# Gate and up projections as one wide product with the high and low halves of x side by side; x loaded first, relative bias by a row-shifted copy in DRAM

## The chip, the cores and the metric

One core of one Trainium2 chip runs the whole program. The metric is the device time of one execution in microseconds, the median of several; lower is better. A difference of under about 0.2% is not one that these measurements tell.

## The reference

Two transformer stacks one after the other on x of 256 tokens by 1024: `first_block` with two layers, `second_block` with one. Six times in all a SwiGLU feed-forward layer runs, and it is most of the work:

```python
x = x + 0.5 * swiglu(rmsnorm(x, g), w_gate, w_up, w_down)   # 1024 -> 2816 -> 1024
```

Between them stand a short convolution with sliding-window attention, a block attention (MoBA) whose 256 keys here are one own block, two cross attentions on a memory of 256 rows that is normed once, a convolution module with gated linear attention, and a last gated projection. Two of the attentions add a relative bias, `table[bucket(query - key)]`, by head.

## The kernel before

**Weights.** All of them stream from DRAM once, in units of 1 MB (`units`, 256 columns or 256 rows of a matrix), into three raw slots. Every unit is two halves. ACT copies a half to `w_hi` (`split`, L480, type fp32r), and DVE subtracts that from the raw values to `w_lo` (`split`, L837); six halves fit in `w_hi` and `w_lo`. Activations are kept the same way, as `xT_hi`, `xT_lo`. A product is three matmuls, hi·hi, hi·lo and lo·hi (`products`, L1347), so that the lost part of each operand is made good. SP issues the load of a unit when `lo_ready` says that the unit three before has been split. ACT may write a half when the half six before it has been used (`half_done`).

**A feed-forward layer** (`ffn`, L1487; `ffn_step` on ACT and DVE) has 11 steps j of 256 hidden columns. For each, PE makes two halves of gate and two of up (`gate_up`, `transposed`): output is hidden by tokens, 128x256 for a half, 24 matmuls of 256 columns. Then it makes the down product of the step before (`down`, `row_half`, 24 matmuls of 512 columns). Both halves of gate share one PSUM bank, as do both of up, and the banks alternate with j, so a step never waits for the last one's results. Steps 2 to 9 are a loop of two steps. DVE multiplies the bank by the scale of the norm (L945 gate, L950 up), ACT applies silu (L537), DVE multiplies both (L954), ACT and DVE make `hid_hi` (L541) and `hid_lo` (L959). The first step of a layer is an `opening`: K tiles 0 to 3 of all four halves first, then 4 to 7, since the tail of x is still being made. After the last step `last_rows` ends the sums one by one; DVE adds each to x (L924), and PE transposes x (L1433) for the next norm. The fifth layer is `late`: x is normed twice first (`final_norm`, L905), and PE broadcasts the scale (`scale_broadcast`, L1482) after the first half of step 1.

**The start.** SP issues the first gate unit, then x, then up and gate; ACT issues gains, table, memory and a few small loads. ACT splits two halves, then makes `xT_hi` (L508), squares x (L492), and splits the next halves. The memory is normed after step 0. After step 1 PE transposes all gain vectors (`memory_and_vectors`, L1565 to L1567) and the memory (L1574), and ACT and DVE make `memT`. Then `relative_bias` reverses the rows of a bias read from DRAM by a matmul with a flipped identity (L1591); DVE copies that out (L981), and only then does the first down product start.

```python
for n, (l, r) in enumerate(((0, 0), (0, 1), (1, 0))):
    last = pe.matmul(dst, lhs[l], rhs[r], start=start and n == 0, stop=stop and n == 2,
```

## Time and profile before

| | |
|---|---|
| median of 3 runs | 1677.15 us (1676.81 to 1677.82) |
| profiled execution, its own time | 1675.95 us |
| its span | 1674.2 us |
| DVE, ACT, POOL busy | 62%, 45%, 4% |
| weight loads of PE (PEld) busy | 89% |
| granted clock of PE, mean | 0.989 |
| moved by DMA | 280.16 MB, 167 GB/s |

Busy PE is the time in which at least one matmul was in flight; matmuls overlap, so the pace of a stream is read from the starts of neighbours in the timeline and not from the duration of one. The chain of waits names the work that set the end. Lines are those of the kernel before.

### The profile page before, as it was taken

What the parts mean: (1) busy time and instruction counts of PE and PEld (TensorE: products, weight loads), DVE (VectorE), ACT (ScalarE), POOL (GpSimd) and SP (SyncE); (2) the same over time, 40 slices, a digit from 0 to 9 for tenths busy, and PEclk for the clock granted to TensorE, in tenths of its full rate; (3) what the DMA queues carried; (4) which work ended last, traced back from release to release, by engine and by line L of the source; (5) the groups of instructions that cost most, each with busy time, mean ns of one, the idle gap of its engine ahead of it and who ended that gap; (6) DMA issues with size and microseconds to landing.
All of it is one profiled execution on the core that took longest, in us unless ns stands there. A gap on an engine that the chain in (4) does not pass through costs nothing.

```text
span 1674.2 us, 27810 instructions
## 1 busy us (share of the span) xinstructions
PE 1612.6 (96%) x11185; PEld 1496.9 (89%) x11185; DVE 1031.4 (62%) x1472; ACT 757.0 (45%) x1009; POOL 70.9 (4%) x142
## 2 busy tenths in 40 slices
PE   6899999999999999999998999999999999999997
PEld 6799989799999899999977999998999898899995
DVE  5655557767555665656466755566555886755565
ACT  4444435445444444444454544444444641544444
POOL 3000001000000000000000800000000000000000
PEclk9999989999999999999999999999999999999999
DMA  7555543535556555555442456546565450456561
GB/s 266 175 179 186 178 138 127 175 126 162 191 178 198 176 183 179 188 181 175 151 159 93 151 176 200 175 159 213 175 200 163 151 176 26 140 194 200 175 206 45
DMA packets 207748, 280.16 MB, mean 167 GB/s; under 512 B 5135, under 2 KB 183721, under 8 KB 207417
## 3 DMA queue, kind: packets, MB, share of 16 engines
q1 hardware_dynamic: 205184, 273.17, 50.1%
q0 software_dynamic: 1040, 3.28, 0.6%
q10 hardware_dynamic: 1448, 2.65, 0.5%
q8 instruction: 54, 0.88, 0.2%
q14 instruction: 22, 0.17, 0.0%
HBM read 276.98 MB, written 2.11 MB: 167 GB/s over the span
## 4 chain that ended last, share of the span: by engine, by line
PE 86%; DVE 10%; ACT 3%; issue 1%; DMA 1%; DVEq 0%; ACTq 0%; SPq 0%
PE bank L1347 79%; DVE w_lo L837 4%; PE bank L1755 2%; PE bank L1433 1%; PE bank L1554 1%; ACT w_hi L480 1%; PE bank L1536 1%; ACT xT_hi L508 1%; DMA x<-in_x 1%; DVE x L924 0%; PE bank L1543 0%; DVE arena L1031 0%; DVE xT_lo L877 0%; PE bank L1591 0%; PE bank L1482 0%
## 5 line engine op out<-in xcount | busy, mean ns | idle before, releaser
L1347 PE MATMUL bank<-xT_hi,w_hi 128*128 128x256 f32 x2512 | 717.9, 286 | 6.1 <-DVE w_lo L837 4.6
L1347 PE MATMUL bank<-xT_lo,w_hi 128*128 128x256 f32 x2512 | 713.1, 284 | 0.0
L1347 PE MATMUL bank<-xT_hi,w_lo 128*128 128x256 f32 x2512 | 713.0, 284 | 0.0
L480 ACT ACTIVATE w_hi<-raw 128x1024 fp32r<-128x1024 f32 x518 | 531.7, 1052 | 289.6 <-PE bank L1347 249.1
L837 DVE TENSOR_TENSOR w_lo<-raw,w_hi 128x1024 fp32r<-128x1024 f32 x518 | 614.4, 1223 | 70.6 <-ACT w_hi L480 70.3
L1347 PEld LDWEIGHTS bank<-xT_hi,w_hi 128*128 128x128 f32 x2512 | 484.3, 193 | 13.9 <-issue 5.9
L1347 PEld LDWEIGHTS bank<-xT_lo,w_hi 128*128 128x128 f32 x2512 | 484.4, 193 | 2.5
L1347 PEld LDWEIGHTS bank<-xT_hi,w_lo 128*128 128x128 f32 x2512 | 484.2, 193 | 0.0
L1347 PE MATMUL bank<-w_hi,hid_hi 128*128 128x512 f32 x528 | 207.9, 394 | 0.8 <-DVE bias L981 0.8
L1347 PE MATMUL bank<-w_lo,hid_hi 128*128 128x512 f32 x528 | 206.2, 391 | 0.0
L1347 PE MATMUL bank<-w_hi,hid_lo 128*128 128x512 f32 x528 | 205.6, 389 | 0.0
L945 DVE TENSOR_TENSOR arena<-bank,scale_row 128x512 f32<-128x512 f32 x66 | 45.6, 691 | 245.8 <-PE bank L1347 245.6
L950 DVE TENSOR_TENSOR arena<-bank,scale_row 128x512 f32<-128x512 f32 x66 | 45.5, 690 | 159.7 <-PE bank L1347 159.7
L541 ACT ACTIVATE hid_hi<-arena 128x512 fp32r<-128x512 f32 x66 | 41.8, 633 | 193.5 <-DVE arena L954 193.5
L1347 PEld LDWEIGHTS bank<-w_hi,hid_lo 128*128 128x128 f32 x528 | 99.2, 188 | 21.1
L1347 PEld LDWEIGHTS bank<-w_hi,hid_hi 128*128 128x128 f32 x528 | 99.4, 188 | 19.9 <-DVE bias L981 1.6
L1347 PEld LDWEIGHTS bank<-w_lo,hid_hi 128*128 128x128 f32 x528 | 99.4, 188 | 17.8
L537 ACT ACTIVATE arena<-arena 128x512 f32<-128x512 f32 x66 | 41.8, 633 | 157.9 <-DVE arena L945 157.9
L1347 PE MATMUL bank<-w_hi,yT_hi 128*128 128x512 f32 x136 | 55.1, 405 | 6.7 <-DVE yT_lo L1045 6.7
L877 DVE SCALAR_TENSOR_TENSOR xT_lo<-bank,cols,xT_hi 128x256 fp32r<-128x256 f32 x88 | 36.4, 477 | 38.8 <-ACT xT_hi L508 38.8
L1347 PE MATMUL bank<-w_hi,yT_lo 128*128 128x512 f32 x136 | 53.1, 390 | 0.0
L1347 PE MATMUL bank<-w_lo,yT_hi 128*128 128x512 f32 x136 | 53.0, 390 | 0.0
(242 smaller groups left out, 1301.6 us busy)
## 6 DMA issues: line engine op xcount, KB each, us to landing
raw<-in_ffn_w_gate SPq DMA_DIRECT2D x44, 1024.0 KB, 5.4
raw<-in_ffn_w_up SPq DMA_DIRECT2D x44, 1024.0 KB, 5.6
raw<-in_ffn_w_down SPq DMA_DIRECT2D x44, 1024.0 KB, 5.0
raw<-in_ffn_w_in SPq DMA_DIRECT2D x44, 1024.0 KB, 5.2
raw<-in_ffn_w_out SPq DMA_DIRECT2D x22, 1024.0 KB, 5.0
raw<-in_w_in SPq DMA_DIRECT2D x10, 1024.0 KB, 5.3
raw<-in_xa_w_kv SPq DMA_DIRECT2D x8, 1024.0 KB, 5.2
raw<-in_od_w_in SPq DMA_DIRECT2D x8, 1024.0 KB, 5.5
```

Of the source, the lines that this page charges most:

```text
L480: act.activation(hi, src, ACT.Copy).then_inc(sem["hi_ready"], 1)
L508: last = act.activation(hi[:, k, :], src, ACT.Copy, scale=gain_of(gain, k))
L537: act.activation(act_gate[:, jb, :], act_gate[:, jb, :], ACT.Silu).then_inc(sem["act_gate_ready"], 1)
L541: act.activation(hid_hi[:, 2 * jb:2 * jb + 2, :], hidden[:, jb, :].rearrange("p (s t) -> p s t", s=2), ACT.Copy).then_inc(sem["hidden_hi_r ...
L837: dve.tensor_tensor(lo, src, hi.bitcast(F32), ALU.subtract).then_inc(sem["lo_ready"], 1)
L877: last = dve.scalar_tensor_tensor(lo[:, k, :], src, gain_of(gain, k), hi[:, k, :].bitcast(F32), ALU.mult, ALU.subtract)
L945: dve.tensor_tensor(halves(act_gate[:, jb, :]), halves(bank[:, 2 * jb, :]), both, ALU.mult)\
L950: dve.tensor_tensor(halves(hidden[:, jb, :]), halves(bank[:, 2 * jb + 1, :]), both, ALU.mult)\
L1347: last = pe.matmul(dst, lhs[l], rhs[r], start=start and n == 0, stop=stop and n == 2, skip_group_check=shared)
L1433: last = pe.transpose(bank[:, k, t * P:(t + 1) * P], x[:, t, k * P:(k + 1) * P], ident[:, :])
L1536: last = pe.matmul(bank[:, g, n * nk:(n + 1) * nk], q_of(h, t), k_of(h, nk), start=True, stop=True)
L1755: last = pe.matmul(bank[:, b, 0:T], tap_diag(tile, j), glu[:, tile, j:j + T], start=j == 0, stop=j == CONV_TAPS - 1)
```

## The change

- `xT_hi` and `xT_lo` become two parts of one buffer `xT` (K tile by part by token), so that both halves of a K tile are 512 adjacent columns. A half of gate or up gets a PSUM bank of its own (n = 0 to 3, no alternation with j). `wide` multiplies `w_hi` of all eight K tiles by the 512 columns, then `w_lo` of all eight by the 256 of `xT_hi`, into the right side of the bank. It waits for `hi_ready` first and for `lo_ready` only before the low part.
- ACT copies the right sides of two banks to `gate_part` and `up_part`, DVE adds the left sides (`gate_sum`, `up_sum`) and then scales. PE waits for `gate_summed` of the step before ahead of half 0, and for `up_summed` ahead of half 2. The splits stand at other places among these instructions.
- `opening` uses `wide_product` (512 and 256 columns by K tile). In the first layer `wide` is used instead, K tiles as x comes in.
- x is loaded first, in two parts, and the first gate unit in two; the memory is loaded on SP after the first up unit. One split instead of two comes before the first norm. The memory is squared and scaled before step 0, and transposed before step 1.
- The other gain vectors are transposed at the end of the first layer (`vectors`), and DVE takes them out after `hid_lo` of its last step (`vector_columns`).
- The bias: POOL copies the spread table in DRAM to 128 rows, each one element further (`shift_dram`), and reads it back strided, once for each attention. Flip, reversal and store are gone.

```diff
+        xT = sb("xT", [P, KD, 2, T], F32R)
+        xT_hi, xT_lo = xT[:, :, 0, :], xT[:, :, 1, :]
...
+            for t, name in enumerate(("x_loaded", "x1_loaded")):
+                sp.dma_start(x[:, t, :], a["x"][0].rearrange("(t p) d -> p t d", p=P)[:, t, :]).then_inc(sem[name], 16)
...
+            pool.dma_start(bass.AP(shift_dram.tensor, 0, [[8 * 512 + 1, P], [512, 8], [1, 384]]),
+                           bass.AP(spread_dram.tensor, 0, [[0, P], [384, 8], [1, 384]])).then_inc(sem["spread_shifted"], 16)
+            pool.wait_ge(sem["spread_shifted"], 16)
+            by_distance = shift_dram[:, :, P - 1:P - 1 + T]
+            pool.dma_start(bias[:, :, :], by_distance).then_inc(sem["bias_loaded"], 16)
...
+                def gate_low():
+                    act.wait_ge(sem["half_done"], plus(g_half + 2, LOOP_HALVES))
+                    act.activation(gate_part[:, :, :], bank[:, 0:2, T:2 * T], ACT.Copy).then_inc(sem["gate_part_ready"], 1)
...
+                gate_low()
+                if j == 0:
+                    up_low()
+                    silu()
+                else:
+                    split(i, base + 2)
+                    silu()
+                    split(i, base + 3)
+                    up_low()
...
                 if j == 0:
                     split(i, base)
+                    gate_sum()
+                    split(i, base + 1)
+                    up_sum()
                     scale_copy(4)
+                    gate_scale()
+                    up_scale()
...
-                ffn_step(f, NJ - 1)
+                ffn_step(f, NJ - 1, after_hidden=vector_columns if n_ffn[0] == 1 else None)
...
-            splits(2)
+            split()
             norm(COL_OF["ffn1"], loaded=True)
-            splits(LEAD - 2)
+            splits(LEAD - 1)
+            memory_scale()
...
+            def wide(v, b, i, first=False):
+
+                pe.wait_ge(sem["hi_ready"], v + 1 if i is None else v + 1 + LOOP_HALVES * i)
+                for k in range(KD):
+                    if first:
+                        c.next("xT_lo_ready")
+                    pe.matmul(bank[:, b, :], w_cols(v, k)[0], xT[:, k, :, :], start=k == 0, stop=False)
+                split_ready(v, i)
+                for k in range(KD):
+                    last = pe.matmul(bank[:, b, T:2 * T], w_cols(v, k)[1], xT_hi[:, k, :], start=False, stop=k == KD - 1)
                 last.then_inc(sem["half_done"], 1)
...
-                        transposed(v + n, gate_up_dst(j, n), X, i)
+                        if n in (0, 2):
+                            ready = j0 + j
+                            pe.wait_ge(sem["up_summed" if n else "gate_summed"], ready if i is None else ready + 2 * i)
+                        wide(v + n, n, i)
...
+                if n_ffn[0] == 1:
+                    memory()
                 gate_up(1)
                 if n_ffn[0] == 1:
-                    memory_and_vectors()
-                    relative_bias()
+                    c.next("xT_lo_ready", 4)
...
                 down(NJ - 2, v0 + 6 * (NJ - 1) + 2)
+                if n_ffn[0] == 1:
+                    vectors()
                 down(NJ - 1, v0 + FFN_HALVES - 2)
```

How PE's rows move in the loop body, first half of gate of a step. Before (six of its 24 rows; the pattern repeats by K tile):

```order
L1347 MATMUL bank<-xT_hi,w_hi 128x256 [waits lo_ready]
L1347 MATMUL bank<-xT_lo,w_hi 128x256
L1347 MATMUL bank<-xT_hi,w_lo 128x256
L1347 MATMUL bank<-xT_hi,w_hi 128x256
L1347 MATMUL bank<-xT_lo,w_hi 128x256
L1347 MATMUL bank<-xT_hi,w_lo 128x256
```

The three matmuls of a K tile stand together, and the half waits for `w_lo`. Now, the whole half:

```order
L1452 ISA [waits gate_summed]
L1456 MATMUL bank<-xT,w_hi 128x512 [waits hi_ready]
L1456 MATMUL bank<-xT,w_hi 128x512 x7
L1459 MATMUL bank<-xT,w_lo 128x256 [waits lo_ready]
L1459 MATMUL bank<-xT,w_lo 128x256 x7
```

Eight matmuls of 512 columns and eight of 256 take the place of 24 of 256; the half now waits for a sum of DVE.

DVE in the loop body of the change, one step from its first split (L971 and L975 are the sums, L979 and L983 the scalings, L1004 the product of gate and up, L1007 `hid_lo`):

```order
L863 TENSOR_TENSOR w_lo<-raw,w_hi 128x1024 [waits hi_ready]
L970 ISA
L971 TENSOR_TENSOR arena<-bank,arena 128x512 [waits gate_part_ready]
L861 REGISTER_ALU
L863 TENSOR_TENSOR w_lo<-raw,w_hi 128x1024 [waits hi_ready]
L979 TENSOR_TENSOR arena<-arena,scale_row 128x512 [waits gate_summed]
L861 REGISTER_ALU
L863 TENSOR_TENSOR w_lo<-raw,w_hi 128x1024 [waits hi_ready]
L975 TENSOR_TENSOR arena<-bank,arena 128x512 [waits up_part_ready]
L983 TENSOR_TENSOR arena<-arena,scale_row 128x512 [waits up_summed]
L1004 TENSOR_TENSOR arena<-arena 128x512 [waits act_gate_ready,up_scaled]
L1007 TENSOR_TENSOR hid_lo<-arena,hid_hi 128x512 [waits hidden_hi_ready]
```

Six instructions of 128x512 stand where there were four, and the third and fourth split now stand ahead of the sum of up, where they stood behind the product of gate and up.

PE in the first layer, between step 1 and the first down product. Before:

```order
L1565 MATMUL bank<-ident,gain_row 128x1 [waits gain_loaded,vectors_loaded]
L1565 MATMUL bank<-ident,gain_row 128x1 x7
L1566 MATMUL bank<-ident,arena 128x128
L1567 MATMUL bank<-ident,arena 128x126
L1574 MATMUL bank<-ident,arena 128x128 [waits scale_ready,cols_ready,mem_normed]
L1574 MATMUL bank<-ident,arena 128x128 x15
L1591 MATMUL bank<-arena 128x512 [waits bias_rev_loaded,xT_lo_ready]
L1591 MATMUL bank<-arena 128x512 x3
L1347 MATMUL bank<-w_hi,hid_hi 128x512 [waits lo_ready,hidden_lo_ready,bias_ready]
```

In the change the sixteen memory transposes stand ahead of step 1, and the last row is:

```order
L1394 MATMUL bank<-w_hi,hid_hi 128x512 [waits lo_ready,hidden_lo_ready,xT_lo_ready]
```

The rows of L1591 are gone, and those of the gain vectors have moved to the end of the layer, ahead of its last down product.

## Rows read from the trace of the kernel before

**Rows 1.** Page, part 1: busy time of PE, share of the span, instructions.

```profile
PE 1612.6 (96%) x11185; PEld 1496.9 (89%) x11185; DVE 1031.4 (62%) x1472; ACT 757.0 (45%) x1009; POOL 70.9 (4%) x142
```

**Rows 2.** Timeline, PE, a loop step: start, duration in us; 21 and 54 matmuls apart.

```profile
430.06 0.39 PE L1347 MATMUL bank<-w_hi,hid_lo 128*128 128x512 f32 x1
...
434.83 0.39 PE L1347 MATMUL bank<-w_hi,hid_lo 128*128 128x512 f32 x1
...
436.01 0.28 PE L1347 MATMUL bank<-xT_hi,w_lo 128*128 128x256 f32 x1
...
442.49 0.28 PE L1347 MATMUL bank<-xT_hi,w_lo 128*128 128x256 f32 x1
```

**Rows 3.** Timeline, PE, at the start, before the clock rose; six matmuls apart.

```profile
14.22 0.41 PE L1347 MATMUL bank<-xT_hi,w_lo 128*128 128x256 f32 x1
...
15.50 0.42 PE L1347 MATMUL bank<-xT_hi,w_lo 128*128 128x256 f32 x1
```

**Rows 4.** Timeline, DVE, a loop step of the third layer; in brackets what it waited for.

```profile
602.79 0.69 DVE L950 TENSOR_TENSOR arena<-bank,scale_row 128x512 f32<-128x512 f32 x1 [2.46 <-PE bank L1347]
...
614.62 2.35 DVE L837 TENSOR_TENSOR w_lo<-raw,w_hi 128x1024 fp32r<-128x1024 f32 x2
...
619.77 0.69 DVE L950 TENSOR_TENSOR arena<-bank,scale_row 128x512 f32<-128x512 f32 x1 [2.80 <-PE bank L1347]
```

**Rows 5.** Timeline, ACT, the same step.

```profile
616.89 1.06 ACT L480 ACTIVATE w_hi<-raw 128x1024 fp32r<-128x1024 f32 x1 [0.57 <-PE bank L1347]
...
621.23 0.63 ACT L541 ACTIVATE hid_hi<-arena 128x512 fp32r<-128x512 f32 x1 [3.27 <-DVE arena L954]
```

**Rows 6.** Timeline, DVE, then PE, end of the first layer.

```profile
209.72 0.69 DVE L950 TENSOR_TENSOR arena<-bank,scale_row 128x512 f32<-128x512 f32 x1 [2.80 <-PE bank L1347]
...
217.42 1.28 DVE L924 SCALAR_TENSOR_TENSOR x<-bank,x 128x512 f32<-128x512 f32 x2
...
218.16 0.66 PE L1433 MATMUL bank<-ident,x 128*128 128x128 f32 x4 [0.29 <-DVE x L924]
```

**Rows 7.** Chain of waits from 0 to 60 us: start, duration in us, what.

```profile
1.32 8.80 DMA x<-in_x
...
16.61 1.16 ACT arena L492 x2
...
21.64 8.93 PE bank L1347 x60
...
31.01 12.94 PE bank L1347 x108
...
43.95 0.59 PE bank L1565 x8
...
50.56 5.25 PE bank L1591 x8
...
56.59 3.47 PE bank L1347 x14
```

**Rows 8.** Busy time by engine from 15 to 20 us; the last two: DMA share, GB/s.

```profile
15.00:20.00 5.00, 2.85 (x20) 2.65 (x18) 3.07 (x16) 4.10 (x8) 5.00 (x11) 1.00 1.09 361
```

**Rows 9.** Timeline, PE, the memory's transposes.

```profile
45.67 1.94 PE L1574 MATMUL bank<-ident,arena 128*128 128x128 f32 x16 [0.76 <-issue]
```

**Rows 10.** Timeline, ACT and then DVE, in the first 45 us.

```profile
12.52 3.02 ACT L508 ACTIVATE xT_hi<-bank,cols 128x256 fp32r<-128x256 f32 x8 [4.02 <-PE bank L1433]
...
41.65 1.42 DVE L1051 TENSOR_SCALAR arena<-arena,small 128x1024 f32<-128x1024 f32 x2
```

**Rows 11.** Timeline, DVE, then PE, steps 0 and 1 of the fifth layer.

```profile
1132.20 1.22 DVE L837 TENSOR_TENSOR w_lo<-raw,w_hi 128x1024 fp32r<-128x1024 f32 x1
...
1132.34 0.70 PE L1482 MATMUL bank<-diag,unit_sq 128*128 128x256 f32 x2 [1.01 <-DVE diag L896]
...
1139.86 0.39 PE L1347 MATMUL bank<-xT_hi,w_hi 128*128 128x256 f32 x1 [0.37 <-DVE w_lo L837]
```

**Rows 12.** Page, part 6: issues of a weight unit, KB each, us to landing.

```profile
raw<-in_ffn_w_gate SPq DMA_DIRECT2D x44, 1024.0 KB, 5.4
```

More of the change, by code:

```diff
@@ L65 @@
 N_COLS = _at
+FIRST_COLS = 24
 def bucket_starts():
@@ L955, in ffn_step @@
                     .then_inc(sem["hidden_ready"], 1)
-                for n in range(2, 4 if j else 2):
-                    split(i, base + n)
                 dve.wait_ge(sem["hidden_hi_ready"], plus(f.j0 + j + 1, 2))
@@ L977, in ffn @@
                 if n_ffn[0] == 1:
-                    memory_norm()
-                    for n in range(4):
-                        c.next("bias_psum")
-                        dve.tensor_copy(bias[:, 2 * n:2 * n + 2, :], halves(bank[:, 4 + n, :]))\
-                            .then_inc(sem["bias_ready"], 1)
+                    xT_los(COL_OF["mem"], memT_hi, memT_lo, by_bank=True)
                 if n_ffn[0] == 6:
@@ L1357, in _, with opening @@
             X, Y, MEM, HID = (xT_hi, xT_lo), (yT_hi, yT_lo), (memT_hi, memT_lo), (hid_hi, hid_lo)
-            def opening(parts, before_last=None, loaded=False):
-                for n, (v, dst, start) in enumerate(parts):
+            def opening(vs, product, before_last=None):
+                for n, v in enumerate(vs):
                     split_ready(v, None)
-                    if n == 2 and not loaded:
+                    if n == 2:
                         rest_of_x()
@@ L1368, in opening @@
                             c.next("xT_lo_ready")
-                        products(dst, w_cols(v, k), xk(X, k), start and k == 0, False, shared=True)
-                for n, (v, dst, _) in enumerate(parts):
-                    if n == len(parts) - 1 and before_last is not None:
+                        product(n, k)
+                for n in range(len(vs)):
+                    if n == len(vs) - 1 and before_last is not None:
                         before_last()
```

191 lines of the change are left out of this document (108 added, 83 removed), and 2 rows, old and new, of the table AX.

## The prediction

> **What bounds the kernel now.** I read the page's busy times first: PE has a matmul in flight for 1612.6 of 1674.2 us [rows 1], so time can come from two places only, a faster stream of matmuls or the few stretches in which PE stands. The timeline of PE gives the stream's pace. Twenty-one matmuls of 512 columns take 434.83 - 430.06 = 4.77 us, 227.1 ns each; fifty-four of 256 columns take 442.49 - 436.01 = 6.48 us, 120.0 ns each [rows 2]. At 2.4 GHz the columns alone need 213.3 and 106.7 ns. So either length pays about 13.5 ns over its columns. At the start, with the granted clock at 1.2 GHz, six matmuls of 256 take 1.28 us, 213.3 ns each, which is the columns and nothing more [rows 3]. A step of a layer lasts 619.77 - 602.79 = 16.98 us [rows 4], and 96 x 0.1200 + 24 x 0.2271 = 16.97 us accounts for it: in the loop PE never waits, and DVE and ACT wait for it [rows 4, 5].
> The chain of the first 60 us shows the other place. x lands at 10.12; two squares on ACT end at 17.77; PE takes up its third half at 21.64; its second step ends at 43.95; then come vectors, memory and bias, and the first down product starts at 56.59 [rows 7].
>
> **Part 1, wide gate and up.** For each K tile of a half, three matmuls of 256 (0.3600 us) become one of 512 and one of 256 (0.2271 + 0.1200 = 0.3471 us). That is 0.0129 us by 32 K tiles in a step by 66 steps: **27.2 us less**. Columns stay the same; 2112 fixed costs go. Low end 0, if the fixed cost comes back in another form, high end 28; I take the rows' value, since both lengths are seen at full clock with a new weight load for each matmul.
> What it adds: on DVE two sums of 0.69 us a step, on ACT two copies of 128x512 at 0.63 [rows 4, 5]. DVE then needs 6 x 0.69 + 6 x 1.18 = 11.2 us and ACT 4 x 0.63 + 6 x 1.0 = 8.5 of a step that is now 16.55. Order matters more than sums. With a step's first wide matmul at 0, halves end at 2.8, 5.6, 8.3 and 11.1, the down halves at 13.8 and 16.6. ACT copies gate at 5.6 to 6.2 and splits until 7.2; DVE sums gate by 6.9, splits until 8.4, scales until 9.1; silu ends at 9.8, ACT's fourth split at 10.8, DVE's at 12.0; ACT copies up at 11.1 to 11.7; DVE sums, scales and multiplies until 14.1; `hid_hi` ends at 14.8, `hid_lo` at 15.5. Now the waits. PE wants the gate sum at 16.6 (9.6 us to spare) and the up sum at 22.1 (9 to spare). `hid_lo` is wanted 16.6 us after the step's end. The last two splits end at about 17.1 and 18.3 and are wanted at 24.9 and 27.7. A raw slot is asked for at 0.7 of the next step at the latest, lands after 5.4 us [rows 12] and is split at 9.8. So the single set of banks costs the loop nothing; the 9 us from bank to sum are its cover.
>
> **Part 2, the ends of the layers.** There `hid_lo` is wanted after one down product, at 16.6, with 1 us to spare, and it holds. But DVE's splits come behind it and the residual behind those. Before, up is scaled at 209.72 and the residual starts at 217.42, and PE waits 0.29 us for it [rows 6]. Now a copy and a sum come first (1.3 us) while two splits (2.35) have gone ahead; ACT's sixth and seventh splits still wait for PE's halves. By hand the residual is 0.2 us later: five ends, **1.0 us more** (0 to 5).
> In the first layer the ten vector transposes, 0.96 us [rows 7], stand ahead of the last down product, and DVE waits for them behind `hid_lo` before its last three splits. On the old scale the step ends at about 209.6 and its down product 24 x 0.2271 = 5.45 later, at 215.0; the vectors end at 216.0. DVE: copies to 216.7, splits to 220.2, residual to 220.9 where it was 218.1: **2.8 us more** (1 to 4).
>
> **Part 3, the fifth layer.** PE must now have the gate sum before it starts step 1. DVE is late there: both norms end in the split at 1132.20, on which the first PE wait ends [rows 11]. The sum comes out at about 1134.1; PE, which had done the first half by 1132.34 - 1.01 = 1131.33 (so from 1128.4 on) and then waited 1.01 us for the scale, starts there. Four halves (11.1) and the broadcast (0.45) end at 1145.7. Before, the fourth half began at 1139.86 [rows 11] and ended at 1142.75. So 2.95 us more, and the 0.8 that Part 1 counts for the two steps is lost as well: **3.8 us more** (0 to 6).
>
> **Part 4, the start.** DMA moved 361 GB/s between 15 and 20 us [rows 8], some 2.8 us a MB. In the new order, at that pace from about 2 us on, x lands by 5.5 us, the first half of gate by 7, its second by 8.2, up by 11, memory by 14, the next gate by 17. PE transposes x by 8.1, ACT's first split ends at 8.0, so `xT_hi` starts at 8.1 where it was 12.52 [rows 10]: 4.4 us. Squares end at 13.3, DVE's norm at 16.1. Half 0 is wide already from 9.6 on, since it needs `w_lo` only for its low part; half 1 ends at 18.2, half 3 at 24.2 (before 32.45: the 108 matmuls from 31.01 hold 12 of the opening [rows 7]). Then a new wait. The memory's transposes need `scale_row`, and that stands on DVE behind memory scaling (1.42 us [rows 10]), two splits and both sums. The second of those splits needs the up unit of step 1, whose load can be issued only after half 1 is split at 17.2 and lands at about 23. I get the scale at 28.7, the transposes (1.94 us [rows 9]) to 30.7, step 1 to 41.9. `memT` is made beside it. Allow 0.7 us for a clock that the idle stretch may lower: the down product starts at 42.6 instead of 56.59, which is 14.0 us, less 0.8 in Part 1: **13.2 us less**. High end 18, if the scale comes with no wait; low end 6, if loads come as late as x did before. The matmuls of the bias (5.25 us [rows 7]) are among what goes. The two strided reads and the copy in DRAM are wanted only at the attentions, some 200 us later and beyond; nobody waits.
>
> **Sum.** 1674.2 - 27.2 + 1.0 + 2.8 + 3.8 - 13.2 = 1641.4 us of span. The profiled execution lies 1.75 above its span and the median 1.2 above that: 1644.3, say **1644 us**.
>
> **A rule of the Trainium skill against it.** The Trainium skill, TensorE: Matmul & The Clock Gate, section on "Wait — 56ns, not 53.3ns?", has a warm matmul cost its columns plus about 2.5 ns, and a cold one exactly its columns. Rows 3 agree with the second; rows 2 show 13.5, not 2.5. By that rule 2112 matmuls would be worth 5.3 us and the time would be 1666.
>
> **Rivals.**
> A. The fixed cost is not saved: it belongs to reading a new K tile or to crossing a bank, and grows with the wide operand. For it: no row shows 512 and 256 columns alternating in blocks in one bank. Against: the down product at 227.1 changes its bank by every third matmul. It gives 1644 + 27 x (0.7 to 1) = 1663 to 1671. Chance 0.07. By the 2.5 ns of the Trainium skill (same page and section) the time is 1666, inside this case.
> B. The start is short of data: the split of gate into rows of 512 bytes, with the DRAM copy beside it, makes units late and the start gains 2 to 7 us. Time 1650 to 1656. Chance 0.09.
> C. More is gained: the scale is early, PE's late waits vanish behind hi-first order. Time 1632 to 1637. Chance 0.08.
> D. Slower. ACT's copy of up waits for PE's fourth half, and `hid_hi` and two splits are queued behind it; if that circle is longer than a step, PE waits in each. It decides when a wanted split is 7.6 us later than I found; to undo 33 us it must go on for 0.6 us in most of the 54 loop steps. Time 1680 or more. Chance 0.02. Against it: DVE and ACT wait 2 to 5 us at a time for PE now [rows 4, 5].
> E. The time stays, because what PE gains in the loop it waits for weights. 1674 to 1680, chance 0.02.
>
> **Numbers.** The forecast's own case, 1637 to 1651, has 0.72. The range takes in B and most of C: 1635 to 1657. Faster by over 0.2% (3.4 us, about what a measurement of this kernel can tell) 0.96, within 0.2% 0.02, slower 0.02.
>
> **What would show it.** Starts of L1456 227 ns apart and of L1459 120 ns; a loop step of 16.55 us; some 9100 matmuls; no PE wait for a sum of DVE save in the fifth layer (about 6 us there); PE idle 4 us near 24 to 29 us for the scale; the first down product at 42 to 43; the first layer's residual 3 us after its down product's second group. Part 1 is wrong if wide matmuls are over 235 ns apart, Part 4 if the down product starts after 48.

## The result, and the profile after

| | before | after |
|---|---|---|
| median of 4 runs, us | 1677.14 (1676.81 to 1677.82) | 1650.93 (1649.44 to 1651.7) |
| ratio of after to before | | 0.9842, 95% interval 0.9825 to 0.9859 |
| profiled execution, span, us | 1674.2 | 1650.0 |

The change is 26.2 us faster. The forecast was 1644 with a range of 1635 to 1657: its sign and range hold, and its middle is 6.9 us too low. One execution of all those reported here, the 1762.46 us of e4_scale_first, fell in a slower state of the chip, at a mean granted clock of 0.845, and the ratios leave it out. The head of the page after (engine, busy time, share of the span, instructions):

```profile
PE 1586.0 (96%) x9065; PEld 1384.2 (84%) x9065; DVE 1135.1 (69%) x1600; ACT 826.0 (50%) x1141; POOL 73.4 (4%) x139
```

PE has a matmul in flight for 26.6 us less [rows 1]; 9065 matmuls answer to the forecast's 9100. DVE and ACT, the engines behind it, still have slack.

**The loop.** The chain of waits of the kernel after, one loop step of the third layer (start, duration, what):

```profile
604.50 5.47 PE bank L1394 x24
609.97 1.81 PE bank L1456 x8
611.78 0.95 PE bank L1459 x8
612.74 1.84 PE bank L1456 x8
614.58 0.95 PE bank L1459 x8
...
621.12 0.93 PE bank L1394 x4
```

From one down product to the next it is 621.12 - 604.50 = 16.62 us, against 16.98 [rows 4] and a forecast of 16.55. A half takes 2.79: eight wide matmuls at 0.230 and eight narrow ones at 0.119. No wait stands between them, so the single set of banks does cost the loop nothing.

**The start.** Timelines of the first 48 us after; first ACT, then PE (start, duration, instruction, in brackets the idle time before it and what ended it):

```profile
10.08 1.06 ACT L493 ACTIVATE w_hi<-raw 128x1024 fp32r<-128x1024 f32 x1 [6.59 <-DMA raw<-in_ffn_w_gate]
11.04 3.01 ACT L521 ACTIVATE xT<-bank,cols 128x256 fp32r<-128x256 f32 x8
...
20.20 1.06 ACT L493 ACTIVATE w_hi<-raw 128x1024 fp32r<-128x1024 f32 x1 [1.08 <-DMA raw<-in_ffn_w_gate]
...
25.87 1.06 ACT L493 ACTIVATE w_hi<-raw 128x1024 fp32r<-128x1024 f32 x1 [1.44 <-DMA raw<-in_ffn_w_up]
```

```profile
5.40 3.67 PE L1504 MATMUL bank<-ident,x 128*128 128x128 f32 x16 [0.28 <-DVE cols L1107]
13.01 3.43 PE L1456 MATMUL bank<-xT,w_hi 128*128 128x512 f32 x8 [3.93 <-DVE xT L903]
...
31.07 3.65 PE L1657 MATMUL bank<-ident,arena 128*128 128x128 f32 x16 [3.67 <-DVE scale_row L940]
34.37 3.03 PE L1456 MATMUL bank<-xT,w_hi 128*128 128x512 f32 x8
37.23 1.12 PE L1459 MATMUL bank<-xT,w_lo 128*128 128x256 f32 x8
38.19 2.00 PE L1456 MATMUL bank<-xT,w_hi 128*128 128x512 f32 x8
```

x is there at 5.4, as forecast, and transposed by 9.1. But on ACT the hi part of x stands behind the first weight copy, whose data lands at 10.05 and not at 7, so it starts at 11.04 instead of 8.1. The second gate unit is late as well: ACT still waits for it before 20.20, where the forecast had it landed by 17. The forecast's pace for these loads, 361 GB/s from about 2 us on, was not met: the windows below have 192 and 229 GB/s in the first 10 us. The next expected thing is there too: PE waits 3.67 us for the scale. Then comes what the forecast priced too low, a low clock. Windows of the kernel after (stretch; busy us and count of PE, weight loads, DVE, ACT, POOL; granted clock, DMA share, GB/s):

```profile
0.00:5.00 5.00, 0.14 (x1) 0.17 (x1) 0.00 (x0) 1.28 (x1) 1.45 (x9) 1.00 0.56 192
5.00:10.00 5.00, 3.80 (x17) 3.28 (x17) 0.18 (x1) 0.00 (x0) 1.40 (x12) 1.00 0.80 229
30.00:35.00 5.00, 3.93 (x18) 3.87 (x19) 3.85 (x7) 2.49 (x4) 0.26 (x1) 0.50 0.97 244
```

At a granted clock of 0.50 (1.2 GHz) the sixteen transposes take 3.65 us where they took 1.94 [rows 9], and the half after them ends 38.19 - 34.37 = 3.82 after its start and not 2.79. The first down product starts at 46.57; it was 56.59 [rows 7].

**End of the first layer, and a wait that nobody touched.** Waits of PE from 195 to 235 us, after (total, times, longest, in us), then a window behind the second of them:

```profile
PE bank L1394 <- DVE w_lo L863: 2.4, 1, 2.4
PE bank L1504 <- DVE x L950: 2.1, 1, 2.1
```

```profile
232.00:236.00 4.00, 4.00 (x20) 4.00 (x20) 1.95 (x2) 0.00 (x0) 0.00 (x0) 0.50 1.06 353
```

At the end of the layer PE waits 2.1 us for the residual, where it waited 0.29 before [rows 6]; that is the cost of the vectors that was forecast. The other wait, 2.44 us for a split in the block between the first and the second layer (until 230.00), stands in the kernel before too, with the same length (until 240.67). Behind it the granted clock is 0.50 from 231 to 244.5 us, with PE busy all the time, and in the kernel before from 242 to 255. By that length it may cost some 6 to 7 us (an estimate: half of the 13 us at half the clock), about as much as the largest gain of an experiment below. It changes nothing in the comparison, and no run here tried to remove it or shows that the wait is what lowers the clock.

**The fifth layer.** Timeline of PE at its opening, after, and the window of the same place:

```profile
1112.50 3.78 PE L1456 MATMUL bank<-xT,w_hi 128*128 128x512 f32 x8 [5.79 <-DVE arena L971]
...
1117.79 0.92 PE L1553 MATMUL bank<-diag,unit_sq 128*128 128x256 f32 x2
1118.28 2.26 PE L1456 MATMUL bank<-xT,w_hi 128*128 128x512 f32 x8
...
1126.92 0.40 PE L1394 MATMUL bank<-w_hi,hid_hi 128*128 128x512 f32 x1
```

```profile
1112.00:1116.00 4.00, 3.50 (x8) 2.81 (x9) 2.18 (x3) 0.00 (x0) 0.00 (x0) 0.50 0.71 238
```

PE waits 5.79 us for the gate sum (about 6 were forecast), and here too comes back at 1.2 GHz: its first half and the broadcast take 1118.28 - 1112.50 = 5.78, where 2.79 and some 0.4 were due.

**Where the 24.2 us of span went.** The marks are the starts of the first and the last down-product matmul of each layer in the two traces (before: 56.59, 222.05; 412.61, 577.96; 602.59, 767.95; 950.23, 1115.58; 1142.83, 1308.19; 1469.01, 1634.36. After: 46.57, 211.38; 401.56, 563.75; 587.73, 749.92; 931.83, 1094.03; 1126.92, 1288.97; 1447.65, 1609.84).

| stretch | after less before, us |
|---|---|
| start to the first mark | -10.0 |
| first layer, mark to mark | -0.7 |
| layers 2 to 6, mark to mark | -16.0 (3.2 each) |
| from layer 1 to 2, 2 to 3, 3 to 4 | -1.4 |
| from layer 4 to 5 (opening and step 1 of the fifth) | +5.6 |
| from layer 5 to 6 | -2.1 |
| tail | +0.3 |

Of the -2.1 some 1.5 is no work of the change: behind the same wait of 1.8 us for a scale, in both kernels, the kernel before had a granted clock of 0.79 between 1316 and 1324 us, and after had 1.00 at the same place of the work.

### The profile page after: what moved, and what is told of

Same layout as the page of the kernel before. It is cut to its first block, busy times and chain, and to the rows that moved or that the text cites. A ratio compares the mean times of both kernels' runs of the same rounds, so it can differ in the third digit from the quotient of the medians.

```text
span 1650.0 us, 23804 instructions
## 1 busy us (share of the span) xinstructions
PE 1586.0 (96%) x9065; PEld 1384.2 (84%) x9065; DVE 1135.1 (69%) x1600; ACT 826.0 (50%) x1141; POOL 73.4 (4%) x139
## 4 chain that ended last, share of the span: by engine, by line
PE 84%; DVE 10%; ACT 3%; issue 1%; DMA 1%; DVEq 0%; SPq 0%; ACTq 0%
PE bank L1394 36%; PE bank L1456 26%; PE bank L1459 13%; DVE w_lo L863 4%; PE bank L1445 2%; PE bank L1831 2%; ACT w_hi L493 1%; PE bank L1504 1%; PE bank L1634 1%; PE bank L1616 1%; ACT xT L521 1%; PE bank L1444 1%; DMA raw<-in_ffn_w_gate 1%; DVE x L950 0%; PE bank L1623 0%
## 5 line engine op out<-in xcount | busy, mean ns | idle before, releaser
L1456 PE MATMUL bank<-xT,w_hi 128*128 128x512 f32 x1952 | 492.1, 394 | 9.7 <-DVE arena L971 5.8
L1456 PEld LDWEIGHTS bank<-xT,w_hi 128*128 128x128 f32 x1952 | 357.6, 190 | 77.4 <-DVE arena L971 6.1
L1459 PEld LDWEIGHTS bank<-xT,w_lo 128*128 128x128 f32 x1952 | 267.1, 191 | 20.3 <-DVE w_lo L863 1.2
L1459 PE MATMUL bank<-xT,w_lo 128*128 128x256 f32 x1952 | 273.1, 283 | 0.8 <-DVE w_lo L863 0.8
L1394 PE MATMUL bank<-xT,w_hi 128*128 128x256 f32 x800 | 148.8, 288 | 0.8 <-DVE xT L903 0.6
L1394 PEld LDWEIGHTS bank<-xT,w_hi 128*128 128x128 f32 x800 | 126.6, 194 | 3.4 <-issue 3.1
L1394 PE MATMUL bank<-xT,w_lo 128*128 128x256 f32 x400 | 114.1, 285 | 0.0
L550 ACT ACTIVATE arena<-bank 128x512 f32<-128x512 f32 x66 | 39.3, 595 | 85.0 <-PE bank L1459 83.9
L971 DVE TENSOR_TENSOR arena<-bank,arena 128x512 f32<-128x512 f32 x66 | 45.5, 690 | 51.4 <-ACT arena L550 51.4
L1007 DVE TENSOR_TENSOR hid_lo<-arena,hid_hi 128x512 fp32r<-128x512 f32 x66 | 46.0, 697 | 46.1 <-ACT hid_hi L572 46.1
L1394 PEld LDWEIGHTS bank<-xT,w_lo 128*128 128x128 f32 x400 | 77.7, 194 | 0.0
L1394 PE MATMUL bank<-w_hi,xT 128*128 128x256 f32 (+2 forms) x288 | 65.0, 320 | 2.8 <-DVE w_lo L863 2.7
```

The costliest lines, as they stand in the source:

```text
L550: act.activation(gate_part[:, :, :], bank[:, 0:2, T:2 * T], ACT.Copy).then_inc(sem["gate_part_ready"], 1)
L971: dve.tensor_tensor(gate, bank[:, 0:2, 0:T], gate_part[:, :, :], ALU.add).then_inc(sem["gate_summed"], 1)
L1007: dve.tensor_tensor(hid_lo[:, 2 * jb:2 * jb + 2, :], hidden[:, jb, :].rearrange("p (s t) -> p s t", s=2), hid_hi[:, 2 * jb:2 * jb + 2, :]. ...
L1456: pe.matmul(bank[:, b, :], w_cols(v, k)[0], xT[:, k, :, :], start=k == 0, stop=False)
L1459: last = pe.matmul(bank[:, b, T:2 * T], w_cols(v, k)[1], xT_hi[:, k, :], start=False, stop=k == KD - 1)
```

## The experiments

My theory: each matmul has a fixed cost that a wider one saves, and the missing 7 us stand mostly in three waits in front of PE, two of them with a low clock behind them. Twelve kernels tell its parts from their rivals. The tables give medians with the lowest and highest run; the ratio is to the kernel before, run beside them on the same chip (median 1674.54 us for the first four, 1677.31 for the next four, 1676.87 for the last). Times and spans are compared with the change's 1650.93 and 1650.0; but the kernel before moved by up to 2.8 us between these groups of runs, so where a difference is under 3 us, the marks of the trace decide. Lines of an edit that stand elsewhere are left out at `...`.

### 1. Wide or narrow, and in which order

**e1_narrow.** Everything of the change stays, but the wide matmul of K tiles 1 to 7 is two of 256 columns (1848 matmuls more):

```diff
-pe.matmul(bank[:, b, :], w_cols(v, k)[0], xT[:, k, :, :], start=k == 0, stop=False)
+if k == 0:
+    pe.matmul(bank[:, b, :], w_cols(v, k)[0], xT[:, k, :, :], start=True, stop=False)
+else:
+    pe.matmul(bank[:, b, 0:T], w_cols(v, k)[0], xT_hi[:, k, :], start=False, stop=False)
+    pe.matmul(bank[:, b, T:2 * T], w_cols(v, k)[0], xT_lo[:, k, :], start=False, stop=False)
...
```

(The openings' `wide_product` is split in the same way.)

> The change with the wide matmul taken back alone: in each half the product of w_hi with both parts of x stays one matmul of 512 columns for K tile 0 and becomes two of 256 for K tiles 1 to 7; banks, partial copies and sums stay. Theory (each matmul pays some 11 to 13 ns over its columns, so what the loop gained is the number of matmuls): 28 more matmuls a step, a loop step of 16.9 us against 16.61, the time 17 to 22 us above the change, 1668 to 1673. Rival (the gain comes from the order or the single banks, not from the count): a step of 16.6 and the time within 3 us of 1651.

**e2_alternate.** The wide and the narrow matmul of a K tile follow each other in the steps, in place of eight and eight:

```diff
-for k in range(KD):
-    pe.matmul(bank[:, b, :], w_cols(v, k)[0], xT[:, k, :, :], start=k == 0, stop=False)
 split_ready(v, i)
 for k in range(KD):
+    pe.matmul(bank[:, b, :], w_cols(v, k)[0], xT[:, k, :, :], start=k == 0, stop=False)
     last = pe.matmul(bank[:, b, T:2 * T], w_cols(v, k)[1], xT_hi[:, k, :], start=False, stop=k == KD - 1)
```

> The change with the 512 and the 256 column matmul of each K tile next to each other again in the loop, as its openings have them, w_lo waited for at the start of a half. The openings of the change show 0.354 us a K tile against 0.349 in the blocked halves. Theory (a 512 column matmul between 256 column ones costs more than among its own kind): a loop step of 16.61 + 32 x 0.005 = 16.77 us, the time 8 to 11 us above the change, about 1660. Rival (the order does not matter, only the count): step 16.61, the time within 2 us of 1651. In the first layer the waits for w_lo return, up to 1 us.

| | time, us | ratio (95%) | span |
|---|---|---|---|
| e1_narrow | 1670.97 (1668.57 to 1673.05) | 0.998 (0.997 to 0.999) | 1669.0 |
| e2_alternate | 1662.33 (1661.01 to 1663.01) | 0.9923 (0.9906 to 0.994) | 1661.2 |

Timeline of PE in e1_narrow, a half in the loop's third layer:

```profile
616.58 0.39 PE L1461 MATMUL bank<-xT,w_hi 128*128 128x512 f32 x1
616.81 0.28 PE L1463 MATMUL bank<-xT,w_hi 128*128 128x256 f32 x1
...
617.04 0.28 PE L1463 MATMUL bank<-xT,w_hi 128*128 128x256 f32 x1
...
618.48 1.12 PE L1467 MATMUL bank<-xT,w_lo 128*128 128x256 f32 x8
619.44 0.40 PE L1461 MATMUL bank<-xT,w_hi 128*128 128x512 f32 x1
```

One K tile as two matmuls takes 617.04 - 616.81 = 0.23 to 0.24 us, and a half is 619.44 - 616.58 = 2.86 long. Rival A, that the fixed cost is not saved, falls: 1848 matmuls of unchanged columns cost 19.0 us of span, 10.3 ns each. From mark to mark a layer takes 165.19 us, 3.00 more than the change's 162.19, which is 11.9 ns for each of its 252 added matmuls; of the 3.16 that the change gained there nearly all is gone, while the new start, banks and sums stay. Every matmul of these traces has a weight load of its own (9065 of each in the page after), so this doesn't tell whether the matmul or its weight load costs the time. The Trainium skill, TensorE: Matmul & The Clock Gate, section "Wait — 56ns, not 53.3ns?", gives about 2.5 ns for a warm matmul over its columns. By that figure it would be 4.6 us (an estimate); this case's trace does not agree, and the measurement decides.

e2_alternate, the same place:

```profile
614.60 0.40 PE L1457 MATMUL bank<-xT,w_hi 128*128 128x512 f32 x1
614.84 0.28 PE L1458 MATMUL bank<-xT,w_lo 128*128 128x256 f32 x1
614.96 0.40 PE L1457 MATMUL bank<-xT,w_hi 128*128 128x512 f32 x1
...
617.43 0.40 PE L1457 MATMUL bank<-xT,w_hi 128*128 128x512 f32 x1
```

Eight K tiles take 617.43 - 614.60 = 2.83 us, 0.354 each, against 2.79 in two blocks. From mark to mark a layer is 163.79 long and not 162.19; with six layers that makes some 10 of the 11.2 us by which the span is longer. The first layer loses 1.6 us more than the others, and there the earlier wait for `w_lo` may count as well. So "all high parts, then all low parts" is worth about 10 us by itself. Why is open, and alternation alone is not the reason: in the opening of the second layer of the change, which still alternates, eleven K tiles in a row take 388.00 - 384.18 = 3.82 us, 0.347 each.

### 2. The gate sum of the fifth layer

**e3_late_sum.** ACT's copy of the low gate part moves ahead of the second squares, and DVE's gate sum ahead of the second norm's small instructions, behind `final_norm`:

```diff
 # ACT
...
 norm("both")
+act.wait_ge(sem["half_done"], late_v0 + 2)
+act.activation(gate_part[:, :, :], bank[:, 0:2, T:2 * T], ACT.Copy).then_inc(sem["gate_part_ready"], 1)
...
 # DVE
 link(dve.tensor_copy(first_rstd, rstd))
+dve.wait_ge(sem["gate_part_ready"], 4 * NJ + 1)
+dve.tensor_tensor(halves(act_gate[:, 0, :]), bank[:, 0:2, 0:T], gate_part[:, :, :], ALU.add)\
+    .then_inc(sem["gate_summed"], 1)
...
```

(At the old places both are skipped for this layer.)

> The change with ACT's copy of gate and DVE's sum of gate moved, in the fifth layer alone, ahead of the second norm's squares and rsqrt, where DVE stands idle 1.2 us; nothing else. Theory (PE's 5.79 us wait at 1112.50 is for that sum, and the low clock after it costs 2.7 us more than the wait itself was forecast to): PE goes on at about 1107.2, waits under 1 us for the scale and up to 2 us for a w_lo, and the time falls 5 to 8 us, to 1643 to 1646. Rival (the norm chain itself sets the end of step 1, so the wait only moves to the scale): under 3 us less, as in the kernel before.

Measured: 1644.14 us (1641.68 to 1646.8), ratio 0.9817 (0.9797 to 0.9837), span 1642.6. Timeline of PE:

```profile
1106.37 2.11 PE L1464 MATMUL bank<-xT,w_hi 128*128 128x512 f32 x8 [0.70 <-DVE arena L939]
1108.32 1.11 PE L1467 MATMUL bank<-xT,w_lo 128*128 128x256 f32 x8
1109.65 0.70 PE L1561 MATMUL bank<-diag,unit_sq 128*128 128x256 f32 x2 [0.22 <-DVE diag L926]
...
1116.64 2.12 PE L1464 MATMUL bank<-xT,w_hi 128*128 128x512 f32 x8 [0.71 <-ACT w_hi L493]
...
1119.55 0.40 PE L1402 MATMUL bank<-w_hi,hid_hi 128*128 128x512 f32 x1
```

The wait shrinks from 5.79 to 0.70 and the half runs at full clock. From the fourth layer's last mark to the fifth's first it is 1119.55 - 1093.0 = 26.55 us, against 32.89 in the change and 27.25 before: 6.3 less. The wait gives 5.1 of it and the clock 2.4 (half and broadcast took 5.78 and now take 3.63, of which 0.22 is a wait). Two waits that come up instead, 0.22 and 0.71, take 0.9 back, the second for a split of ACT, and some 0.3 is not traced.

### 3. The start

**e4_scale_first.** In the first step of the first layer DVE copies `scale_row` ahead of the splits and sums, since the memory's transposes wait for it:

```diff
 if j == 0:
+    if f.j0 == 0:
+        scale_copy(4)
     split(i, base)
...
-    scale_copy(4)
+    if f.j0 != 0:
+        scale_copy(4)
```

> The change with the copy of scale_row, in the first layer alone, ahead of the two splits and sums of DVE's step 0. Theory (PE waits 3.67 us for scale_row behind two splits and two sums, then transposes and the first half of step 1 run at the low clock): transposes start at about 27.6 us where they start at 31.07, at full clock, and the first down product at 41 to 42 where it is 46.57; the time 4 to 6 us less, 1645 to 1647. Rival (the second split's weights, which land at 25.9, or the gate sum hold PE as well): the gain is under 2 us.

**e5_one_load.** The first gate unit comes in one load of 1 MB, where the change has two of 512-byte rows:

```diff
-if u == 0:
-    sp.dma_start(dst[:, :, 0:P], src[:, :, 0:P]).then_inc(sem["first_half_loaded"], 16)
-    sp.dma_start(dst[:, :, P:UC], src[:, :, P:UC]).then_inc(raw_ready[slot], 16)
-    return
...
```

> The changed kernel with the first gate unit in one load of 1 KB rows instead of two halves of 512-byte rows. Theory (the two halves with their short rows move slowly: 192 and 229 GB/s in the first 10 us against 171 and 384 before, and the first half lands 8.3 us after its issue): the whole unit lands at 8.5 to 9.5 us, the hi half of the normalised x starts 1 to 1.5 us before its 11.0, and the down products start at 45 to 45.5 instead of 46.57, the total 1 to 1.5 us under the change. Rival (the bytes in front of it set the landing, not the row length): a whole unit is twice the bytes of its first half, lands near 11, the scalar engine starts nothing sooner, and the down products start at 46.5 to 48, the total 0 to 1.5 us over the change. Second rival (nothing of the first opening matters, since the first wide product waits for the vector engine's row scale anyway, 3.67 us): down products at 46.5 in either case.

**e6_w_before_x.** As e5_one_load, with x's two loads issued behind that unit.

> As the run with one load, and x loaded behind the first gate unit, as the kernel before had it; everything else of the change stands. Theory (x first is what lets the norm's mean squares start early, and the norm sets when hi is there): the first mean square waits some 2 us longer, the hi half of x starts at 12 to 12.5, down products start 1.5 to 2 us later than in the run with one load, and the total is 1.5 to 2 us over it. Rival (the start is set by the row scale behind the vector engine's own work, not by x's landing): down products within 0.5 us of the run with one load.

**e9_one_copy_late.** As e5_one_load; POOL's copy inside DRAM waits for the twelfth half:

```diff
 pool.wait_ge(sem["spread_stored"], 16)
+pool.wait_ge(sem["half_done"], 12)
```

> As the run with one load of the first gate unit (1658.7 us, down products at 54.56), and the copy of the bias inside DRAM, which now waits until the twelfth gate or up half is done (near 80 us; the bias is first used after the first layer). There the up unit was issued at 22.4, one us behind the copy's 21.4, and landed 12.6 us later, so that the tensor engine waited 9.9 us; in the change it was issued at 20.1, ahead of the copy, and landed in 5.7. Theory (the 8 us that one load cost are the up unit behind the copy): the unit lands 5 to 6.5 us after its issue, the wait at the transposes of the memory is 4 to 6 us again, down products at 47.5 to 49.5, total 5 to 7 us under that run's. Rival (the one load makes the opening late by itself, through the order of the weight buffers): down products stay at 53 or later.

**e10_x_hi_first.** The change with the hi part of the first x ahead of the first weight copy on ACT, and the lo part ahead of the first split on DVE:

```diff
+xT_his(COL_OF["ffn1"], xT_hi)
 split()
 act.wait_ge(sem["x_loaded"], 16)
 act.wait_ge(sem["x1_loaded"], 16)
-norm(COL_OF["ffn1"], loaded=True)
+mean_square(0)
+mean_square(1)
...
```

> The changed kernel with the hi and lo parts of the first normalised x ahead of the first weight copy and split, on the scalar and the vector engine. Theory (x is there at 5.4 us and transposed by 9.1, but its hi part waits to 11.0 behind a weight copy whose data lands at 10.05, so loading x first brings nothing in the change's own order): the hi part starts at 6 to 7, the first wide product at 11 to 11.5 instead of 13.0, the up unit is issued 1 to 2 us earlier, down products at 44.5 to 46, total 1 to 2 us under the change. Rival (a wait further back, on the vector engine's queue of splits or on the second gate unit's landing, takes the time back): first wide product early, down products at 46.3 to 46.8.

**e11_copy_late.** The change with the same wait on POOL alone.

> The changed kernel with only the copy inside DRAM held back to the twelfth half. Theory (in the change as it stands the copy costs the start nothing that the tensor engine sees: the up unit is ahead of it, and the unit that took 12 us beside it was waited for 0.96 us by the scalar engine alone): down products at 46 to 46.8, the unit issued at 28.4 lands in 5.5 to 7 instead of 12, total within 0.7 us of the change. Rival (the copy's traffic slows splits or loads that the opening rests on): down products 1 us or more earlier.

| | time, us | ratio (95%) | hi part of x | first wide product | wait for the scale | first down product |
|---|---|---|---|---|---|---|
| the change | 1650.93 (1649.44 to 1651.7) | 0.9842 (0.9825 to 0.9859) | 11.04 | 13.01 | 3.67 | 46.57 |
| e4_scale_first | 1646.56 (1645.36 to 1762.46) | 0.9831 (0.9812 to 0.9851) | | | 0.23 | 40.80 |
| e5_one_load | 1658.68 (1657.75 to 1660.22) | 0.989 (0.987 to 0.9909) | 13.30 | 15.34 | 9.9 | 54.56 |
| e6_w_before_x | 1649.7 (1647.95 to 1650.02) | 0.9833 (0.9814 to 0.9852) | 10.31 | 11.45 | 3.9 | 45.16 |
| e9_one_copy_late | 1652.15 (1650.5 to 1652.65) | 0.985 (0.9833 to 0.9866) | 13.06 | 15.03 | 3.56 | 47.55 |
| e10_x_hi_first | 1650.64 (1650.36 to 1651.54) | 0.9845 (0.9829 to 0.9862) | 7.80 | 11.82 | 5.62 | 45.81 |
| e11_copy_late | 1650.14 (1648.02 to 1651.81) | 0.9837 (0.9821 to 0.9853) | 11.37 | 13.34 | 3.71 | 45.98 |

**The scale.** e4_scale_first, timeline of PE:

```profile
27.75 1.94 PE L1660 MATMUL bank<-ident,arena 128*128 128x128 f32 x16 [0.23 <-DVE scale_row L940]
29.52 2.11 PE L1459 MATMUL bank<-xT,w_hi 128*128 128x512 f32 x8
```

The wait goes, and with it the low clock: 5.8 us for one 0.41 us copy set earlier. Of that 3.3 is the earlier start of the transposes (31.07 - 27.75), 1.5 the transposes and 0.9 the half behind them at full clock.

**x first.** My theory of e6_w_before_x was wrong. With x behind the weights the hi part of x starts at 10.31, earlier than the change's 11.04 and not at 12 to 12.5, and PE starts at 11.45. Timeline of ACT in e6_w_before_x:

```profile
6.54 1.06 ACT L488 ACTIVATE w_hi<-raw 128x1024 fp32r<-128x1024 f32 x1 [2.87 <-DMA raw<-in_ffn_w_gate]
10.31 3.03 ACT L516 ACTIVATE xT<-bank,cols 128x256 fp32r<-128x256 f32 x8 [2.72 <-PE bank L1499]
```

Once the weights are split, ACT has only PE's transposes to wait for. In the change's own order of work on ACT, x first moves the wait from x to the weights and no more. (The up unit of step 1 is issued at 19.43 here, ahead of POOL's copy at 22.24; the part on the copy shows why the time is so far below that of e5_one_load.)

That the unit in one load lands late in e5_one_load (its copy starts at 12.34 against 10.08) is the rival's reading: what is issued beside a load counts. In the change SP needs 5.63 us, from 2.84 to 8.47, to issue the up unit behind the two short-rowed halves, and in e5_one_load 0.59 (SP is held 6.69 us by the next issue, that of the memory), so there a further MB shares the DMA engines with x and gate. That the short rows themselves cost something isn't shown.

**The copy in DRAM.** The first down product of e5_one_load is 8.0 us later than the change's, of which the late first unit explains 2.3 at the most, and here is the rest; ACT's timeline, then the windows:

```profile
24.45 1.05 ACT L487 ACTIVATE w_hi<-raw 128x1024 fp32r<-128x1024 f32 x1
35.07 1.06 ACT L487 ACTIVATE w_hi<-raw 128x1024 fp32r<-128x1024 f32 x1 [9.57 <-DMA raw<-in_ffn_w_up]
```

```profile
20.00:25.00 5.00, 4.84 (x27) 3.92 (x27) 4.86 (x10) 4.97 (x8) 2.29 (x4) 1.00 0.44 133
25.00:30.00 5.00, 4.69 (x29) 4.01 (x27) 4.62 (x15) 0.50 (x1) 0.00 (x0) 1.00 0.99 205
```

The up unit of step 1 was issued at 22.42, one us behind POOL's copy of 1.5 MB (21.4), and landed after 12.6 us, with the DMA engines 0.99 busy at 205 GB/s. In the change it was issued at 20.14, ahead of the copy (21.4), and was split at 25.87, 5.7 us later. e9_one_copy_late puts the copy at 59 us and nothing else:

```profile
27.61 1.06 ACT L488 ACTIVATE w_hi<-raw 128x1024 fp32r<-128x1024 f32 x1 [2.36 <-DMA raw<-in_ffn_w_up]
```

```profile
32.98 2.83 PE L1652 MATMUL bank<-ident,arena 128*128 128x128 f32 x16 [3.56 <-DVE scale_row L935]
```

Issued at 22.15, there in 5.4 us; down product at 47.55 and not 54.56. So 7.0 us hung on the copy. It does no such harm in the change as it stands, where the unit is issued 1.3 us ahead of it. The Trainium skill, DMA: Bandwidth & Descriptors, section "Queues, rings and completion order", says that a DMA engine takes turns between the queues that have work, a packet at a time. A load beside the long copy takes about twice as long here, which fits; no run shows the turns themselves. e11_copy_late shows the rest of it: the unit that took 12.0 us beside the copy (issued at 28.4) takes 6.4 without it. But nobody on PE's path wanted it, and the total stays the same.

**What can't be told apart.** Five runs with the change's own start (the change, e1, e2, e3 and e7) have their first down product at 46.57, 46.21, 45.78, 45.75 and 45.53, e1 and e2 with other matmuls in that stretch. In the other three the scale comes at nearly the same time (transposes from 30.98 to 31.14), and what differs is the low clock behind it. The 45.98 of e11_copy_late and the 45.81 of e10_x_hi_first lie in that spread. In e10_x_hi_first the first wide product is 1.2 us earlier for certain, but the wait for the scale is 5.62 instead of 3.67: the scale's copy ends at 30.9 in the change and still at 30.6 here, because DVE makes it behind the memory's norm, whose squares stand on ACT behind the second gate unit (split at 20.20 in the change, at 19.92 here). That was the rival, and it took most of the time back.

### 4. The vectors, and all together

**e7_vectors_behind.** The building of the bias vectors goes behind the last three splits of the first layer's last step:

```diff
-if after_hidden is not None:
-    after_hidden()
 for n in range(4 if j else 2, n_splits):
     split(i, base + n)
+if after_hidden is not None:
+    after_hidden()
```

> The changed kernel with the building of the bias vectors moved behind the last three splits of the first layer's last step. Theory (the 2.5 us by which the first layer's body gains less than the others' is the vectors' copies ahead of the splits in the vector engine's queue, with the tensor engine held once for 2.1 us): the first layer from its first to its last down product takes 162.2 to 162.8 instead of 164.81, the end of the next opening does not move back, total 1.5 to 2.5 us under the change. Rival (the vectors' work is only moved: the second layer's opening or its columns wait for it instead): first layer shorter by 2, the stretch to the second layer longer by as much, total within 0.5 us of the change.

Measured: 1648.3 us (1646.52 to 1648.67), ratio 0.9826 (0.9807 to 0.9845), span 1646.2. Timeline of DVE, the copy of the columns and the residual behind it, first in the change:

```profile
202.71 0.40 DVE L1102 COPY cols<-bank 128x230 f32<-128x230 f32 x1 [2.25 <-PE bank L1648]
203.34 3.50 DVE L863 TENSOR_TENSOR w_lo<-raw,w_hi 128x1024 fp32r<-128x1024 f32 x3
```

and in e7_vectors_behind:

```profile
203.08 0.39 DVE L1102 COPY cols<-bank 128x230 f32<-128x230 f32 x1
203.70 1.42 DVE L950 SCALAR_TENSOR_TENSOR x<-bank,x 128x512 f32<-128x512 f32 x2
```

DVE no longer waits 2.25 us with the splits behind it, and the residual starts 3 us sooner. The first layer is 162.81 from mark to mark instead of 164.81, inside the 162.2 to 162.8 as good as expected, and from there to the second layer's first mark it is 189.9 against 190.2. The 2.0 us are gained and not moved. (Another 1.0 of its span is the start's spread.)

**e8_all.** The edits of e3, e4, e5 and e7 in one kernel.

> The changed kernel with four edits together: the gate sum behind the fifth layer's norm (it gave 7.4 us of span alone), the scale copies of the first step of the first layer ahead of its split (6.4 us), the first gate unit in one load, and the vectors behind the last splits. Theory (they sit in different places and add up): 7.4 + 6.4 + 0 to 1.5 + 1.5 to 2.5, so a span of 1632 to 1635 and a time 15 to 18 us under the change's 1651. Rival (two of them lean on the same wait, as the one load and the scale copies both do at the first wide product): 3 us less of it, span 1636 to 1639.

Measured: 1646.51 us (1645.53 to 1647.38), ratio 0.9815 (0.9797 to 0.9833), span 1645.6. It gains less than both forecasts, and it was laid out before e5's result was known. Its down product starts at 49.85, against 40.80 in e4_scale_first: with one load the up unit is issued at 21.55, again one us behind the copy (20.5), and lands 12.4 us later. The other two parts are there in full: 162.81 for the first layer, 26.55 before the fifth.

**e12_best.** The edits of e3, e4, e7 and e10 and the late copy, without the one load.

> The changed kernel with five edits: the fifth layer's gate sum behind its norm, the scale copies of the first step ahead of the split, the vectors behind the last splits, x's parts ahead of the first weight copy, and the copy inside DRAM held back. No one load. Theory (the four with others' spans: 7.4 - 0.8, 6.4 - 0.6, 3.8 - 1.0 by their places alone, so 6.3 to 6.6, 5.8, 1.9, and 1 to 2 of x's parts): span 1633 to 1635.5, total some 1635 to 1637 or 15 us under the change. Rival (some of the four overlap at the end of the opening): 1638 to 1640.

Measured: **1637.18 us** (1636.0 to 1637.83), ratio 0.9763 (0.9746 to 0.9779), span 1635.5. Timeline of PE at the start, and at the fifth layer:

```profile
27.16 1.94 PE L1671 MATMUL bank<-ident,arena 128*128 128x128 f32 x16 [0.77 <-DVE scale_row L951]
28.93 2.12 PE L1470 MATMUL bank<-xT,w_hi 128*128 128x512 f32 x8
...
1099.14 2.11 PE L1470 MATMUL bank<-xT,w_hi 128*128 128x512 f32 x8 [0.70 <-DVE arena L943]
...
1112.32 0.40 PE L1408 MATMUL bank<-w_hi,hid_hi 128*128 128x512 f32 x1
```

It takes 13.7 us off the change and beats both kernels. Its marks place them: 6.4 us at the start (first mark 40.22, 0.6 better than e4_scale_first alone), 2.0 in the first layer, 6.3 before the fifth.

## Why the prediction was right, and where it was 6.9 us too low

- **The matmul stream (Part 1), right.** 27.2 us were forecast from the fixed cost of 13.5 ns. A loop step gave 0.36, which is 24 us over 66 steps. e1_narrow shows that it is the number of matmuls (3.00 of the 3.16 us a layer). The term was mis-sized by 3 us: behind a narrow block the wide ones start 0.230 apart and not 0.227, so a K tile takes 0.349 and not 0.347. The order of the matmuls has no price in the forecast; alternating, as in e2_alternate, the term would have been some 10 us smaller.
- **Enough cover in the loop, right.** Not one wait of PE in the loop: rivals D and E fall on the chain of waits above.
- **The start (Part 4), right in kind, 4.0 us short.** It gave 10.0 us where 14.0 were forecast. "The first half of gate by 7" failed (10.05), and with it the hi part at 8.1. But e10_x_hi_first shows that this wasn't what counted: the wait that set the end, for the scale, was named, and came 2.4 us later than its 28.7 (transposes from 31.07). One load that it rests on, "the next gate by 17", was still waited for at 20.2: the memory's squares stand behind its split. "Allow 0.7 us for a clock" failed too: from the transposes to the first down product it was 15.50 us, and 13.05 at full clock in e4_scale_first, so the low clock took 2.5. The 2.4 and this 1.8 make the 4.0 within 0.2.
- **The fifth layer (Part 3), right in kind, 2.7 us short.** The wait was forecast at about 6 and was 5.79. That PE comes back from it at 1.2 GHz stands in none of the terms; it is 2.4 to 2.6 us.
- **The ends of the layers and the vectors (Part 2), right.** The first layer gained 2.5 less than the others, where 2.8 were forecast; e7_vectors_behind gives 2.0 of it back.
- **The sum.** 3.3 of the stream, 4.0 of the start and 2.7 of the fifth layer, less the 1.5 of clock that the profiled run before had lost, make 8.5, and the span is 1650.0 - 1641.4 = 8.6 above the forecast. That the run before had lost 1.5 to the clock is luck of one execution, and so is most of the 2 us by which the median is nearer, as it lies 0.9 over the span and not 2.95.
- **The rivals.** B, the start short of data, gives the right time (1650 to 1656) but not its mechanism: it takes 6 to 12 us from the start, and the start missed 4.0. Loads were late as B has it (10.05 and 20.2), and the first wide product stood behind one, but the wait that set the end was for DVE's order, as e4_scale_first shows. e5_one_load is B as it would have looked. C was there to be had, for 13.7 us, mostly by the order of work on DVE.

## What to carry to other kernels

Put as many columns behind each weight load as a bank takes, and the equal ones together: a cost of about 12 ns per matmul is saved, as long as the engines behind keep up, as they did here. Then look at every wait that is left in front of the tensor engine, and at the granted clock behind it: waits of 3.6 to 9.9 us cost their length and 1.5 to 2.6 us of slow clock, and behind one of 2.4 us, in both kernels, the clock was low for 13 us. One small instruction set earlier on the vector engine was worth about 6 us, in two places. A long transfer that nobody wants soon should be held back by a wait of its own, not left to a race with the loads.

## What the runs showed of the hardware

- From the sixteen transposes at the start to the first down product it is 13.05 and 13.06 us after stands of PE of 0.23 and 0.77 (e4, e12), at a granted clock of 1.00. It is 14.55 to 14.61 after stands of 3.56 to 3.86 (e3, e6, e7, e9, e11), 15.50 after 3.67 in the change, and 15.04 and 15.01 after 5.62 and 9.86 (e10, e5). The same work lost 1.5 to 2.5 us to the clock, and not more after a longer stand; part of it can fall behind the transposes, which alone took 2.35 to 3.65 for 1.94.
- A stand of 1.8 us was followed by 0.50 in the kernel before (1321 to 1323) and by 1.00 after; one of 2.06 by 1.00 (after, 208 to 212); one of 2.44 by 0.50 for 13 us in both kernels.
- A 256-column matmul between two of 512 makes a pair of 0.354 us in the loop, and in blocks of eight 0.349. It was worth about 10 us here and is not explained; in the second layer's opening such pairs took 0.347.
- A load of 1 MB took 5.4 to 6.4 us without a copy of 1.5 MB within DRAM in its way (e9, e11) and 12.0 to 12.6 beside it (the change, e8, e5), with the DMA engines 0.99 busy at 205 GB/s.
- SP was held for 5.63 us in the change (6.04 in e11, 3.14 in e10) in issuing one load behind two of 512-byte rows. Behind one of 1 KB rows that took 0.59, and the next load held it for 6.69 (e5).
